# Neighbourhood attention: value products ahead of the next scores, bias tables requested first in each head, on one Trainium2 core

## The chip, the core and the metric

The kernel is one program on one core of a Trainium2 chip. Five instruction streams run side by side and meet only at semaphores: TensorE (PE: matrix products and transposes), VectorE (DVE), ScalarE (ACT), GpSimd (POOL) and SyncE (SP, which here issues DMAs). The metric is device time in microseconds (us) of one execution. All weights and activations are f32; every product is made from halves in a reduced format (high and low, fp32r), usually three matmuls instead of one.

## The reference, cut to what matters

A first transformer block is followed by a second one of two layers. The last attention, changed here, is the neighbourhood attention on 512 tokens (a grid of 8 rows x 64 columns) with 256 context tokens, 16 heads of width 64. Cut from the reference:

```
s_band = einsum('bqhd,brkhd->bhqrk', q_row, kb) * scale + bias      # bias: learned, by 2-D offset
s_band = where(col_mask, s_band, -inf)                             # 16 columns around the query
s_ctx  = einsum('bqhd,bchd->bhqc', q_row, k_c) * scale
p      = softmax(concatenate([s_band, s_ctx], -1))
o      = einsum(p_band, vb) + einsum(p_ctx, v_c)                   # then  y = o @ wo,  h = h + gate * y
```

After it come an RMS norm, a gated FFN, and the last norm.

## The kernel before, in words

**One iteration j (0 to 7) treats two heads of the model.** Below, "head j" is such a pair; h (0, 1) is the member. The 512 queries are cut into four units x of 128 queries (16 columns x 8 rows). `near_steps` (L2741) is the list of steps that all five engines follow. For a unit the steps are:

- `scores j x`: 24 matmuls (L2914, L2917) of 256 columns into PSUM banks 0 to 3: 256 neighbour keys and 256 context keys for each h.
- VectorE reduces them to negated, biased scores and their minimum (`max`, L3096 and L3099, two instructions for each h; the second reads the bias table `tab`). ScalarE takes the exponential with its sum (`exp`, L2992), VectorE its reciprocal (`inv`, L3105), ScalarE multiplies (`share`, L2997).
- `turn j 2x+h`: four transposes (L2928) of the shares into one PSUM bank, from which ScalarE and VectorE take a high and a low half (`t_hi` L528, `t_lo` L533).
- `values j 2p+h`: for a pair p of units, 10 matmuls (L2941) for each h. ScalarE copies one half (`low`, L3014), VectorE adds the other (`full`, L3121), ScalarE and VectorE split the sum (`o_hi` L528, `o_lo` L533).

**Each head has two halves, p = 0 and p = 1.** Between their steps `place` (L539) lays the rest of the work as filler: the projections of head j+1 (`k`, `q`, `v`: L369 to L371; 512 and 256 columns), the transposes of its values (`turn_v`, L2878, halved by `tv_hi` and `tv_lo`), and the output projection of head j-1 (`out`, four steps of two groups n of three matmuls; L369 to L371 from `whi`), whose results VectorE adds to `hT` (L3081). In the first half the order of the steady state is: turns of units 0, `k` 512 columns, turns of unit 1, `k` 256 columns, scores of units 2 and 3, values of p = 0, `q`. In the second: turns of unit 2, `v` 512, turns of unit 3, `out 0`, `v` 256, scores of units 0 and 1 of head j+1, values of p = 1, `out 1`, `out 2`, `turn_v`, `out 3`, and the turns of head j+1.

**PSUM.** Scores own banks 0 to 3. All else shares banks 4 to 7; `Spare` (L588) gives each step the bank that should be free first by the costs in `NEAR_COST`, and `hold` makes TensorE wait until the bank's last reader has gone (`n_add` for `out`, `n_sum` for values, `n_tv_lo` for `turn_v`). In the second half of head 2 the groups n = 2, 3, 4, 5 get banks 5, 6, 7, 5: group 5 waits until VectorE has added group 2.

**Order on the other engines.** `in_time` (L574) sorts the work of ScalarE, VectorE and GpSimd by planned times: the TensorE time of the step plus an offset from `NEAR_SCALAR`, `NEAR_VECTOR`, `NEAR_GPSIMD`. Each engine works strictly in that order.

**Weights and tables.** A step `split` stands for a chunk of weights: SyncE fetches one (L382), ScalarE makes its high half (L394), GpSimd or VectorE the low half (L405). A step `table` fetches the bias rows of a head by 16 small DMAs (L3168) and lets GpSimd make three masked versions for each h (L3149).

**The end.** For head 7 the output projection is done in two strips of 256 queries (`out3`, eight groups each), with the squares for the next norm (`sq` L2241, `sum` L2254) and a product with ones that sums them (`ones`, L2213 and L2215). The order before is: turns, `out3` strip 0, values of p = 1, `ones` 0, `out3` strip 1, `ones` 1; the FFN follows.

Of the kernel before, what the change touches and what calls it, by code (L numbers as in the profile page):

```python
# [373 lines left out]
def fetch_chunk(K, e, w):  # L374

    i = K.fetch_i
    K.fetch_i += 1
    if i >= len(K.chunks):
        return
    if i >= 2:  # L380
        w.wait_ge(*K.at(K.lo_by.get(i - 2, "wlo_dve"), i - 2))
    e.dma_start(K.view(K.raw[i % 2], i), K.chunks[i][0]).then_inc(*K.dma(f"raw{i % 2}", i))  # L382
# [156 lines left out]
def place(fill, share):  # L539

    out = [([], []) for _ in share]
    total, spent, f = sum(c for c, _ in fill), 0.0, 0
    for u in range(len(share)):
        due = total * sum(share[:u + 1]) / sum(share)
        half = total * (sum(share[:u]) + 0.5 * share[u]) / sum(share)
        while f < len(fill) and spent + 0.5 * fill[f][0] < half:
            out[u][0].append(fill[f][1])
            spent += fill[f][0]
            f += 1
        while f < len(fill) and (u + 1 == len(share) or spent + 0.5 * fill[f][0] < due):  # L550
            out[u][1].append(fill[f][1])
            spent += fill[f][0]
            f += 1
    return out
# [2179 lines left out]
def near_load(j):  # L2734

    k = [(0, ("split", j, "k")), (5.4, ("k", j, 0)), (2.8, ("k", j, 512))]
    v = [(0, ("split", j, "v")), (5.4, ("v", j, 0)), (2.8, ("v", j, 512)), (0.7, ("turn_v", j, 0))]
    return k, [(0, ("split", j, "q")), (5.4, ("q", j, 0))], v


def near_steps():  # L2741
    yield "clear", 0, 0
    yield "table", 0, 0
    yield "first_q", 0, 0
    yield "first_k", 0, 512
    yield "second_q", 0, 0
    yield "split_first", 0, "q"
    yield "second_k", 0, 0
    yield "split_first", 0, "k"
    yield "v", 0, 0  # L2750
    yield "scores", 0, 0
    yield "scores", 0, 1
    yield "v", 0, 512
    yield "turn_v", 0, 0
    yield "loop", 0, 0
    for j in range(8):
        k, q, v = near_load(j + 1) if j < 7 else ([], [], [])
        out = [(1.4, ("out", j - 1, n2)) for n2 in range(4)] if j else []
        split = [(0, ("split", j - 1, "out"))] if j else []
        if j < 7:  # L2760
            fill = k + q + [(0, ("table", j + 1, 0))] + v[0:2] + out[0:1] + v[2:3] + split + out[1:3] + v[3:] + out[3:]
            spread = place(fill, NEAR_SHARE)
        else:
            spread = [(split + out[0:1], []), (out[1:2], []), (out[2:4], []), ([], []), ([], []), ([], [])]
            spread = [([s[1] for s in first], []) for first, _ in spread]
        for p in range(2):
            parts = [first + second for first, second in spread[3 * p:3 * p + 3]]
            for h in range(2):
                yield "turn", j, 4 * p + h
            yield from parts[0]  # L2770
            for h in range(2):
                yield "turn", j, 4 * p + 2 + h
            yield from parts[1]
            if p == 0 or j < 7:
                for u in range(2):
                    yield "scores", j + p, 2 * (1 - p) + u
            else:
                yield "out3", 7, 0
            for h in range(2):
                yield "values", j, 2 * p + h  # L2780
            yield from parts[2]
    yield "split_first", 7, "out"
    yield "ones", 7, 0
    yield "out3", 7, 1
    yield "ones", 7, 1


NEAR_SHARE = [1, 0.5, 1, 1, 0.5, 1]
NEAR_COST = {**END_COST, "first_q": 2.9, "first_k": 5.8, "second_q": 2.9, "second_k": 2.9, "q": 5.4, "turn_v": 0.8, "out": 1.4, "scores": 0.95,
             "turn": 0.45, "values": 1.2}  # L2790

# [43 lines left out]
def near_tensor(K, e, w):  # L2835
    wqkv, wo = K.A["na_wqkv_2"][0], K.A["na_wo_2"][0]
    held, spare = {}, Spare(near_steps(), near_cost, near_chain)
    K.named("n_start")
    for what, j, x in spare:
# [111 lines left out]
def near_scalar(K, e, w):  # L2951
    def bank(*key):
        return K.bank(K.xbank[("n",) + key])
    for what, j, x in in_time(near_steps(), near_cost, NEAR_SCALAR, near_chain):
        (qh, ql), (kh, kl), vv = K.nq[j % 2], K.nk[j % 2], K.nv[j % 2]
        if what == "split":
# [85 lines left out]
def near_vector(K, e, w):  # L3042
    def bank(*key):
        return K.bank(K.xbank[("n",) + key])
    for what, j, x in in_time(near_steps(), near_cost, NEAR_VECTOR, near_chain):
        (qh, ql), (kh, kl), vv = K.nq[j % 2], K.nk[j % 2], K.nv[j % 2]
        if what == "split":
# [108 lines left out]
def near_sync(K, e, w):  # L3156
    fetch_chunk(K, e, w)
    w.wait_ge(*K.at("wlo_dve", K.chunk_of["n_start"] - 1))
    for what, j, x in near_steps():
        if what == "table":  # L3160
            w.wait_ge(*K.was("n_max", j - 2, 3, 1))
            if j == 1:
                w.wait_ge(*K.at("norm_lo", "n", KC - 1, 2))
            for h in range(2):
                t = K.tab[j % 2][h][:, 0, :].rearrange("p (r q) -> p r q", q=32)
                for r in range(8):
                    rows = bass.AP(K.rpbd, ((2 * j + h) * 15 + r) * 128 + 40, [[1, 16], [128, 8], [1, 32]])
                    e.dma_start(t[16 * r:16 * r + 16, :, :], rows).then_inc(*K.dma(f"table_in{h}", j, r))  # L3168
        elif what in ("split", "split_first"):
            if K.fetch_i > K.chunk_of["n_end"]:  # L3170
                w.wait_ge(*K.at("n_max", 6, 3, 1))
            fetch_chunk(K, e, w)
# [60 lines left out]
def sync_program(K, e, w):  # L3233
    f0, f1, f2 = feeds(K)
    prelude_sync(K, e, w)
    mixers_sync(K, e, w)
    mixed_sync(K, e, w)
    ffn_sync(K, e, w, f0)
    tail_sync(K, e, w, f0)
    diff_sync(K, e, w)  # L3240
    ffn_sync(K, e, w, f1)
    tail_sync(K, e, w, f1)
    near_sync(K, e, w)
    ffn_sync(K, e, w, f2)
    tail_sync(K, e, w, f2)
# [103 lines left out]
```

## Time and profile before

| | us |
|---|---|
| median of 3 runs | 2666.27 |
| lowest, highest | 2665.56, 2669.49 |
| the profiled execution | 2657.69 |
| its span | 2655.9 |
| TensorE busy | 2474.9 (93%) |
| VectorE busy | 1564.7 (59%) |
| ScalarE busy | 1060.6 (40%) |
| GpSimd busy | 321.1 (12%) |

The span runs from the first to the last instruction that the profile records. The profiled execution took 1.8 us more than its span, and is itself 8.6 us under the median of the three runs. TensorE carries the kernel. The neighbourhood attention lies between about 1865 and 2286 us of the span; there TensorE is busy for 368.6 us of 421.

### The profile page before, as it was taken

The page shows a single profiled execution, that of the slowest core. Times are in us where ns is not written, and L with a number is a line of the kernel's source. Part 1 is how long each engine was busy: PE and PEld are TensorE (multiplying, and loading weights), DVE is VectorE, ACT ScalarE, POOL GpSimd, SP SyncE. Part 2 cuts the span into 40 slices and gives each one's busy share as a digit, 9 for nine tenths or more (in the row PEclk, how much of TensorE's full clock was granted, in tenths as well). Part 3 has the DMA queues.
Part 4 walks back from the last instruction along what each step waited for, and adds up shares of the span by engine and source line. Part 5 has one row for each costly group of instructions (what it writes and reads, how often), then busy time and mean ns, then how long its engine had stood idle before and what let it go on. Part 6 is the DMA issues. An engine that isn't in the chain of part 4 may idle for free.

```text
span 2655.9 us, 35953 instructions
## 1 busy us (share of the span) xinstructions
PE 2474.9 (93%) x14147; PEld 2127.4 (80%) x14147; DVE 1564.7 (59%) x3016; ACT 1060.6 (40%) x1888; POOL 321.1 (12%) x231
## 2 busy tenths in 40 slices
PE   7999989999997999998799999999889988899998
PEld 6888777788787877786688888889878877788887
DVE  4555556878877777777756444445645456533334
ACT  5455534222235655555621211213555555422223
POOL 2122100000012222211100000001232322000001
PEclk9999889999998999999899999999999999899999
DMA  4111023455441111111133333331122211232231
GB/s 122 41 48 48 25 96 111 155 166 182 153 136 48 33 41 40 35 38 48 48 104 122 109 107 127 100 121 55 44 50 55 52 52 52 76 99 95 94 112 49
DMA packets 236577, 218.56 MB, mean 82 GB/s; under 512 B 26164, under 2 KB 205146, under 8 KB 236410
## 3 DMA queue, kind: packets, MB, share of 16 engines
q1 hardware_dynamic: 236410, 216.27, 26.6%
q8 instruction: 113, 1.85, 0.3%
q14 instruction: 54, 0.44, 0.1%
HBM read 214.01 MB, written 2.22 MB: 81 GB/s over the span
## 4 chain that ended last, share of the span: by engine, by line
PE 73%; DVE 13%; ACT 8%; issue 5%; POOL 1%; SPq 0%; DMA 0%; DVEq 0%; POOLq 0%; ACTq 0%
PE ps L369 23%; PE ps L370 22%; PE ps L371 22%; ACT whi L394 1%; DVE FR L533 1%; PE ps L2476 1%; PE ps L2928 1%; ACT FA L2569 1%; DVE FA L667 1%; DVE hT L2649 1%; ACT FR L528 1%; DVE wlo L405 1%; DVE FA L2689 1%; ACT FA L2997 1%; PE ps L2941 1%
## 5 line engine op out<-in xcount | busy, mean ns | idle before, releaser
L369 PE MATMUL ps<-Uh,whi 128*128 128x512 f32 (+2 forms) x2544 | 899.6, 354 | 17.9 <-ACT FA L2588 5.9
L370 PE MATMUL ps<-Ul,whi 128*128 128x512 f32 (+2 forms) x2544 | 885.2, 348 | 0.0
L371 PE MATMUL ps<-Uh,wlo 128*128 128x512 f32 (+2 forms) x2544 | 884.9, 348 | 0.0
L369 PEld LDWEIGHTS ps<-Uh,whi 128*128 128x128 f32 x2544 | 488.6, 192 | 83.1 <-issue 13.7
L371 PEld LDWEIGHTS ps<-Uh,wlo 128*128 128x128 f32 x2544 | 487.2, 191 | 59.6
L370 PEld LDWEIGHTS ps<-Ul,whi 128*128 128x128 f32 x2544 | 488.5, 192 | 57.2
L394 ACT ACTIVATE whi<-raw 128x1024 fp32r<-128x1024 f32 (+2 forms) x205 | 296.5, 1447 | 530.2 <-PE ps L371 530.0
L405 DVE TENSOR_TENSOR wlo<-raw,whi 128x2048 fp32r<-128x2048 f32 (+2 forms) x121 | 248.4, 2053 | 264.3 <-ACT whi L394 264.1
L369 PE MATMUL ps<-FR,whi 128*128 128x512 f32 (+1 forms) x864 | 301.1, 349 | 14.4 <-DVE wlo L405 4.8
L370 PE MATMUL ps<-FR,whi 128*128 128x512 f32 (+1 forms) x864 | 298.3, 345 | 0.0
L371 PE MATMUL ps<-FR,wlo 128*128 128x512 f32 (+1 forms) x864 | 297.9, 345 | 0.0
L405 POOL TENSOR_TENSOR wlo<-raw,whi 128x1024 fp32r<-128x1024 f32 x84 | 201.5, 2399 | 646.2 <-ACT whi L394 645.5
L533 DVE TENSOR_TENSOR FR<-ps,FR 128x512 fp32r<-128x512 f32 (+7 forms) x284 | 142.4, 533 | 145.8 <-ACT FR L528 144.6
L2169 POOL TENSOR_TENSOR FA<-FA 128x256 f32<-128x256 f32 x63 | 49.9, 806 | 1379.4 <-ACT FA L2049 1378.3
L528 ACT ACTIVATE FR<-FA 128x512 fp32r<-128x512 f32 x100 | 58.4, 584 | 351.6 <-DVE FA L1844 343.5
L667 DVE SCALAR_TENSOR_TENSOR FA<-FA,cond 128x512 f32<-128x512 f32 x280 | 196.9, 744 | 1.3
L369 PEld LDWEIGHTS ps<-FR,whi 128*128 128x128 f32 x864 | 164.2, 190 | 37.1 <-ACT whi L394 4.9
L528 ACT ACTIVATE FR<-ps 128x512 fp32r<-128x512 f32 (+7 forms) x304 | 131.2, 467 | 126.8 <-PE ps L371 78.7
L371 PEld LDWEIGHTS ps<-FR,wlo 128*128 128x128 f32 x864 | 164.2, 190 | 19.8
L370 PEld LDWEIGHTS ps<-FR,whi 128*128 128x128 f32 x864 | 164.3, 190 | 19.3
L369 PE MATMUL ps<-whi 128*128 128x512 f32 (+1 forms) x208 | 86.8, 417 | 48.5 <-DVE hT L3081 28.6
L1844 DVE TENSOR_TENSOR FA<-ps,FA 128x512 f32<-128x512 f32 x88 | 54.8, 623 | 115.9 <-PE ps L371 114.4
(352 smaller groups left out, 3041.0 us busy)
## 6 DMA issues: line engine op xcount, KB each, us to landing
FA<-in_ada_w_dram SPq DMA_DIRECT2D x192, 256.0 KB, 2.8
raw<-in_ffn_w_gate_up_dram SPq DMA_DIRECT2D x44, 1024.0 KB, 5.1
raw<-in_ffn_w_down_dram SPq DMA_DIRECT2D x24, 768.0 KB, 4.2
raw<-in_w_in_dram SPq DMA_DIRECT2D x29, 512.0 KB, 3.9
raw<-in_da_wqkv_dram SPq DMA_DIRECT2D x24, 512.0 KB, 3.7
raw<-in_na_wqkv_dram SPq DMA_DIRECT2D x24, 512.0 KB, 3.7
raw<-in_w_ffn_gate_dram SPq DMA_DIRECT2D x11, 1024.0 KB, 5.3
raw<-in_w_ffn_up_dram SPq DMA_DIRECT2D x11, 1024.0 KB, 5.5
```

The costliest lines, as they stand in the source:

```text
L369: e.matmul(out, ah, bh, start=start, stop=False)
L370: e.matmul(out, ah, bl, start=False, stop=False)
L371: return e.matmul(out, al, bh, start=False, stop=stop)
L394: e.activation(K.view(K.hi[i % 2], i), K.view(K.raw[i % 2], i), ACT.Copy).then_inc(*K.ev("whi", i))
L405: e.tensor_tensor(K.view(K.lo[i % 2], i), K.view(K.raw[i % 2], i), K.view(K.hi[i % 2], i).bitcast(F32), ALU.subtract).then_inc(*K.ev(by, i))
L528: e.activation(hi, src, ACT.Copy, scale=scale).then_inc(*K.ev(*done))
L533: e.tensor_tensor(lo, src, hi.bitcast(F32), ALU.subtract).then_inc(*K.ev(*done))
L667: e.scalar_tensor_tensor(out=o, in0=wv, scalar=K.cond[:, k, c:c + 1], in1=o, op0=ALU.mult, op1=ALU.add).then_inc(*K.ev("ada", i, c))
L1844: e.tensor_tensor(mt, K.bank(4 + m % 2)[:, 0:t1 - t0], K.sil[:, m % 2, 0:t1 - t0], ALU.mult).then_inc(*K.ev("f_mul", st, m))
L2169: e.tensor_tensor(acc, acc, K.st_sq4[:, k, :], ALU.add).then_inc(*K.ev("pool_sum", f.st, n, i, z))
L2476: t = e.matmul(K.ps[:, 1024 * mp + c0:1024 * mp + c0 + a1 - a0], q[r:r + 64, q0:q0 + P], k[r:r + 64, a0:a1], start=n == 0, stop=n == 2)
L2569: e.activation(Pm, Pm, ACT.Exp, bias=st[:, 0:1], scale=-1.0, accum_out=st[:, 1:2]).then_inc(*K.ev("d_exp", j, x, mp))
```

## The change

It exchanges two steps in both halves of each head (values first, then the scores of the next two units), requests the next head's bias table as the first filler of a head, with a wait of SyncE on GpSimd's last table, and changes the shares by which the filler is spread.

```diff
-            fill = k + q + [(0, ("table", j + 1, 0))] + v[0:2] + out[0:1] + v[2:3] + split + out[1:3] + v[3:] + out[3:]
+            fill = [(0, ("table", j + 1, 0))] + k + q + v[0:2] + out[0:1] + v[2:3] + split + out[1:3] + v[3:] + out[3:]
...
             yield from parts[1]
+            for h in range(2):
+                yield "values", j, 2 * p + h
             if p == 0 or j < 7:
                 for u in range(2):
                     yield "scores", j + p, 2 * (1 - p) + u
             else:
                 yield "out3", 7, 0
-            for h in range(2):
-                yield "values", j, 2 * p + h
             yield from parts[2]
...
-NEAR_SHARE = [1, 0.5, 1, 1, 0.5, 1]
+NEAR_SHARE = [0.7, 0.8, 1, 0.7, 0.8, 1]
...
             w.wait_ge(*K.was("n_max", j - 2, 3, 1))
+            w.wait_ge(*K.was("n_table", 2 * j - 1))
```

In the steady heads the filler keeps its places. In head 0 the `k` step of 256 columns moves behind the scores in both versions, so values follow the turns directly after the change. In head 7, `out3` of strip 0 now follows the values.

TensorE, second half of head 2, before. L2914 and L2917 are the scores, L2941 the values, the first row the end of `v`, the last the start of `out 1`.

```order
L371 MATMUL ps<-Uh,wlo 128x256
L2914 MATMUL ps<-FR 128x256 x6
L2917 MATMUL ps<-FR 128x256 x6
L2914 MATMUL ps<-FR 128x256 x6
L2917 MATMUL ps<-FR 128x256 x6
L2941 MATMUL ps<-FR 128x256 x6
L2941 MATMUL ps<-FR 128x128 x4
L2941 MATMUL ps<-FR 128x256 x6
L2941 MATMUL ps<-FR 128x128 x4
L369 MATMUL ps<-whi 128x512
```

The same place after.

```order
L371 MATMUL ps<-Uh,wlo 128x256
L2941 MATMUL ps<-FR 128x256 x6
L2941 MATMUL ps<-FR 128x128 x4
L2941 MATMUL ps<-FR 128x256 x6
L2941 MATMUL ps<-FR 128x128 x4
L2914 MATMUL ps<-FR 128x256 x6
L2917 MATMUL ps<-FR 128x256 x6
L2914 MATMUL ps<-FR 128x256 x6
L2917 MATMUL ps<-FR 128x256 x6
L369 MATMUL ps<-whi 128x512
```

The 20 matmuls of the values now stand ahead of the 24 of the scores. The banks move too: the groups n = 2, 3, 4, 5 now get banks 4, 6, 7, 5, of which 5 is that of the values; `turn_v` gets 4 and 6, the groups 6 and 7 get 5 and 7 (in odd heads with 4 and 5 exchanged).

ScalarE, second half of head 2, before. L2979 is the copy of `v`, L2992 `exp`, L2997 `share`, L394 the chunk's high half, L3014 `low`, L528 from FA `o_hi`, the last two rows `tv_hi`.

```order
L2979 ACTIVATE FA<-ps 128x256
L2992 ACTIVATE FA,stat<-FA,stat 128x512 x4
L2997 ACTIVATE FA<-FA,stat 128x512 x2
L394 ACTIVATE whi<-raw 128x1024
L3014 ACTIVATE FA<-ps 64x256 x2
L2997 ACTIVATE FA<-FA,stat 128x512 x2
L528 ACTIVATE whi<-FA 128x8x32
L528 ACTIVATE FR<-ps 128x4x2x64
L528 ACTIVATE FR<-ps 128x3x2x64
```

The same place after.

```order
L2979 ACTIVATE FA<-ps 128x256
L3014 ACTIVATE FA<-ps 64x256 x2
L528 ACTIVATE whi<-FA 128x8x32
L394 ACTIVATE whi<-raw 128x1024
L2992 ACTIVATE FA,stat<-FA,stat 128x512 x4
L2997 ACTIVATE FA<-FA,stat 128x512 x4
L528 ACTIVATE FR<-ps 128x4x2x64
L528 ACTIVATE FR<-ps 128x3x2x64
```

The copy, its half and the chunk now stand ahead of the exponentials. On VectorE, `full` goes ahead of the four reductions, `o_lo` between those of the two units, and the additions of groups 2 and 3 behind them, ahead of the reciprocals.

VectorE, end of head 7, before. L2269 adds the groups of strip 0, L2254 sums squares, L405 is the low half of the FFN's first chunk, L3121 `full`, L533 from FA `o_lo`.

```order
L2269 SCALAR_TENSOR_TENSOR hT<-ps,mod,hT 128x8x32 x5
L2254 TENSOR_TENSOR FA<-FA 128x256
L2269 SCALAR_TENSOR_TENSOR hT<-ps,mod,hT 128x8x32 x2
L2254 TENSOR_TENSOR FA<-FA 128x256 x2
L405 TENSOR_TENSOR wlo<-raw,whi 128x2048
L3121 TENSOR_TENSOR FA<-ps,FA 64x2x8x16 x2
L533 TENSOR_TENSOR wlo<-FA,whi 128x8x32
```

The same place after.

```order
L2269 SCALAR_TENSOR_TENSOR hT<-ps,mod,hT 128x8x32
L3121 TENSOR_TENSOR FA<-ps,FA 64x2x8x16 x2
L2269 SCALAR_TENSOR_TENSOR hT<-ps,mod,hT 128x8x32 x2
L533 TENSOR_TENSOR wlo<-FA,whi 128x8x32
L2269 SCALAR_TENSOR_TENSOR hT<-ps,mod,hT 128x8x32 x3
L2254 TENSOR_TENSOR FA<-FA 128x256
L2269 SCALAR_TENSOR_TENSOR hT<-ps,mod,hT 128x8x32
L405 TENSOR_TENSOR wlo<-raw,whi 128x2048
L2269 SCALAR_TENSOR_TENSOR hT<-ps,mod,hT 128x8x32
L2254 TENSOR_TENSOR FA<-FA 128x256 x2
```

The chunk's low half now stands ahead of the last addition and of the last two sums of squares, on which `ones` 0 waits; ScalarE has the chunk's high half between its fifth and sixth square. SyncE requests the next table ahead of the chunk fetches of a head instead of behind the second one, and GpSimd makes it behind the first low half of a head instead of behind the third.

## Rows read from the trace of the kernel before

**Rows 1.** Waits of TensorE, 1890 to 2290 us: total, times, longest.

```profile
PE ps L369 <- DVE hT L3081: 28.6, 7, 4.2
```

**Rows 2.** Windows: six second halves (heads 1 to 6), scores start to next projection; sum.

```profile
sum 97.93, PE 73.42 PEld 62.55 DVE 61.56 ACT 56.75 POOL 14.11; mean PE 12.24 PEld 10.42 DVE 10.26 ACT 9.46 POOL 2.35
```

**Rows 3.** Timeline of TensorE, second half of head 2: start, us, instruction, wait.

```profile
2026.17 0.50 PE L2914 MATMUL ps<-FR,whi 64*128 64x256 f32 x4
2027.79 2.52 PE L2941 MATMUL ps<-FR 128*128 128x256 f32 x20
...
2030.15 0.45 PE L369 MATMUL ps<-whi 128*128 128x512 f32 x1
...
2036.49 0.80 PE L369 MATMUL ps<-whi 128*128 128x512 f32 x1 [4.05 <-DVE hT L3081]
...
2042.76 0.47 PE L369 MATMUL ps<-Uh,whi 128*128 128x512 f32 x1
```

**Rows 4.** Timeline of VectorE, the same stretch.

```profile
2027.28 0.42 DVE L3096 CUSTOM_DVE_ANT_0 FA<-ps,zero 128x256 f32<-128x256 f32 x1 [2.33 <-issue]
...
2034.78 0.88 DVE L3121 TENSOR_TENSOR FA<-ps,FA 64x256 f32<-64x256 f32 x2 [2.88 <-ACT FA L3014]
2035.69 1.41 DVE L3081 SCALAR_TENSOR_TENSOR hT<-ps,mod,hT 128x512 f32<-128x512 f32 x2
...
2039.66 1.16 DVE L533 TENSOR_TENSOR FR<-ps,FR 128x512 fp32r<-128x512 f32 x2 [0.73 <-ACT FR L528]
```

**Rows 5.** Timeline of ScalarE, the same stretch.

```profile
2031.61 1.32 ACT L2997 ACTIVATE FA<-FA,stat 128x512 f32<-128x512 f32 x2
2032.83 1.04 ACT L394 ACTIVATE whi<-raw 128x1024 fp32r<-128x1024 f32 x1
2033.90 0.78 ACT L3014 ACTIVATE FA<-ps 64x256 f32<-64x256 f32 x2
...
2039.03 1.13 ACT L528 ACTIVATE FR<-ps 128x512 fp32r<-128x512 f32 x2 [2.69 <-PE ps L2878]
```

**Rows 6.** Windows: us, busy time of the engines, PEclk, DMA share, GB/s.

```profile
2036.49:2042.00 5.51, 5.51 (x17) 4.46 (x18) 4.25 (x7) 1.09 (x2) 0.00 (x0) 0.51 0.32 95
...
1901.40:1903.63 2.23, 0.00 (x1) 0.00 (x1) 0.20 (x2) 2.23 (x6) 0.00 (x0) 1.00 0.01 4
...
1278.70:1281.40 2.70, 0.72 (x3) 0.33 (x3) 0.99 (x3) 1.55 (x4) 0.00 (x0) 0.88 0.00 0
```

**Rows 7.** Timeline of TensorE, first half of head 3.

```profile
2053.77 2.53 PE L2941 MATMUL ps<-FR 128*128 128x256 f32 x20
...
2061.67 0.60 PE L2928 MATMUL ps<-ident,FA 128*128 128x128 f32 x4
```

**Rows 8.** Timeline of VectorE, first half of head 3: the first reduction.

```profile
2054.02 0.41 DVE L3096 CUSTOM_DVE_ANT_0 FA<-ps,zero 128x256 f32<-128x256 f32 x1
```

**Rows 9.** Timeline of ScalarE, first half of head 3: the first shares.

```profile
2058.34 1.32 ACT L2997 ACTIVATE FA<-FA,stat 128x512 f32<-128x512 f32 x2
```

**Rows 10.** Timeline of TensorE, second half of head 0.

```profile
1946.14 1.76 PE L2878 MATMUL ps<-ident,FA 128*128 128x128 f32 x7 [5.90 <-ACT FA L2979]
```

**Rows 11.** Timeline of VectorE, second half of head 0.

```profile
1935.37 0.43 DVE L3096 CUSTOM_DVE_ANT_0 FA<-ps,zero 128x256 f32<-128x256 f32 x1 [5.67 <-POOL FA L3149]
```

**Rows 12.** Timeline of TensorE, head 7 from the last scores.

```profile
2235.19 0.51 PE L2914 MATMUL ps<-FR,whi 64*128 64x256 f32 x4
...
2249.25 0.56 PE L369 MATMUL ps<-whi 128*128 128x256 f32 x1
...
2261.31 0.58 PE L369 MATMUL ps<-whi 128*128 128x256 f32 x1 [4.12 <-DVE wlo L533]
```

**Rows 13.** Timeline of ScalarE, end of head 7.

```profile
2255.34 1.89 ACT L394 ACTIVATE whi<-raw 128x2048 fp32r<-128x2048 f32 x1
```

**Rows 14.** Timeline of VectorE, end of head 7.

```profile
2257.27 2.29 DVE L405 TENSOR_TENSOR wlo<-raw,whi 128x2048 fp32r<-128x2048 f32 x1 [1.05 <-ACT whi L394]
```

**Rows 15.** Timeline of SyncE, head 2: the requests of a table.

```profile
2009.30 9.28 SPq L3168 DMA_DIRECT2D FA<-rpb_rows  x16
```

## The prediction

> **What bounds the kernel now.** I first read the page: TensorE is busy for 93% of the span and is the chain that ended last, so only its waits and its clock can give time back. The view of waits, cut to the attention that is changed, names one large item: seven waits of about 4 us, 28.6 us in all, of a group of the output projection on VectorE's addition [rows 1]. The windows of the six second halves that have it (heads 1 to 6), each from the start of the scores to the next head's projection, sum to 97.93 us, a mean of 16.3 [rows 2]. Then the timelines of one of them, engine by engine. TensorE: scores at 2026.17, values at 2027.79 (1.62 later), `out 1` at 2030.15 (2.36 later); three groups, then 4.05 idle until 2036.49, and from there 6.27 to the next projection [rows 3]. VectorE: the reductions start 1.1 after the scores do; `full` comes only at 2034.78, and the addition that frees the bank at 2035.69 [rows 4]. ScalarE says why: `low` at 2033.90 stands behind the exponentials, a share pair (1.32) and a chunk (1.04) [rows 5]. The wait is thus a bank held through a queue, and values issued earlier could shorten it. Last, the clock: in the 5.5 us behind the wait the granted clock is 0.51, the 1.2 GHz level [rows 6].
>
> **Second halves, heads 1 to 6.** I lay the new order on the durations of rows 3 to 5, with V, the end of `v` (2026.17 in rows 3), as zero. TensorE: values 0 to 2.36, scores to 3.98. ScalarE: `low` 2.47 to 3.25, `o_hi`, chunk to 5.65, then four exponentials at a pitch of about 0.87. VectorE: `full` 3.35 to 4.2; two pairs of reductions at 0.87 to 5.9; `o_lo` to 6.3 (256 columns; 0.35 is an estimate from 1.16 for two of 512 in rows 4); two more to 8.0; additions of groups 2 and 3 (1.41) to 9.4; reciprocals to 9.8; additions 4 and 5 to 11.2. ScalarE's shares then lie at 9.6 to 12.2 (twice 1.32), and `tv_hi` (1.13) at 12.2 to 13.3, since it is queued behind them.
>
> TensorE meanwhile: four groups at 0.69 (2.06 for the three before the wait), to 6.74; group 5 has the bank of the values, free at 4.2, and no longer waits. `turn_v` does: its first bank is that of group 2, added at 8.7, its second that of group 3, 9.4. It waits about 2.05, then 0.2, and ends at 9.9. Group 6 has the bank of group 5, added at 11.2: 1.4 of idle. Groups 6 and 7 end at 12.7. The turns of the next head need the two banks of `turn_v`, halved by VectorE at 13.5 and 14.1: 0.9 and 0.2 idle, ending at 14.6; the next projection has group 6's bank, added at 14.8. It starts at V + 14.9. So one wait of 4.05 becomes some five that sum to nearly 5, none over 2.1; what is saved is what the clock cost.
>
> At full clock a half then takes 14.9 against 16.3: 1.4 saved. Will the clock hold? The trace has both. Through a single wait of 2.23 it stayed at 1.00; in a stretch of 2.70 us with 0.72 busy, ahead of a wait of 1.93, it fell (0.88 in the mean) [rows 6]. Here TensorE is busy for some 3 of the 8 us from V + 6.7 on, nearer to the second row. I take it that it falls in most heads, about 3 us into the stretch. In rows 3 the work behind the wait (6.27) would take about 3.7 at full clock by its own warm groups (three groups at 0.69, and an estimate of 0.1 for each of 15 transposes), so the lower level costs up to 2.6 there. Here most of groups 6 and 7 at the lower level hides behind `tv_hi`; what reaches into turns and projection is 0.2 to 2.5, and I take 0.9. Gain 0.5 a head, 3.0 for six. Bounds: 6 x 1.4 = +8.4 with no fall, 6 x -1.1 = -6.6 with the longest one.
>
> The Trainium skill, "TensorE: Matmul & The Clock Gate", section "A second HAM failure mode: psum-queue depth-cycling", tells of a kernel in which short idle times between groups, from cycling through PSUM banks, made the clock go up and down, with the loss paid between bursts. That speaks against breaking one wait into five; by that rule the six halves would bring nothing or lose, by my 0.9 they still bring 3.0. The row of the 2.23 us wait does not bear it out alone, that of the 2.70 us stretch does.
>
> **First halves, heads 1 to 6.** Before, scores are followed by values and `q`, 7.90 in all, until the turns [rows 7]. The reductions start 1.9 after the scores [rows 8], the shares 4.32 after those [rows 9]. After, the turns have only `q` between: scores end at 3.98, `q` (5.53) at 9.5 from the end of `k`. The reductions start behind `full` at 4.15, `o_lo` adds 0.35, so the first share ends at 4.15 + 4.32 + 0.35 + 0.66 = 9.5, the second at 10.15. The turns wait about 0.3. Cost 6 x 0.3 = -1.8; bounds 0 (the spacing absorbs it) and -0.6 each. The cover of the softmax chain is used up here.
>
> **Head 0.** Here TensorE waited 5.90 for the copy of `v` [rows 10], because the first reduction waited 5.67 for GpSimd's late table [rows 11]. With the table requested two fetches earlier both go. Next in line is ScalarE, with the copy behind `low`, `o_hi`, four exponentials and a share: 10.5 against an arrival of TensorE at 7.0, so 3.9 of waiting with the latency, 2.0 less; and TensorE, whose seven transposes took 1.76 behind the long wait, gets about 0.9 back of the lower level: +2.9. In the first half the values follow the turns with nothing between, and wait 1.2 for `t_lo`; ScalarE has the share of unit 3 and `q` later, which costs the last turn some 0.7 more: -1.9. Together +1.0, bounds -1 and +3.
>
> **Head 7 and the end.** In the first half of head 7 the seventh wait of rows 1 goes and the turns wait for shares and banks. By the schedule above the shares end at 12.2 and the last turn at 13.0 from the start of the values; before it took 14.1 from the start of the scores, 2235.19 to 2249.25 [rows 12]. +1.1 (0 to 2). The end loses. Counted from the last turn (T, 2249.25), strip 1 of `out3` started at T + 12.06 before, after a wait of 4.12 on `o_lo` (rows 12 too). That wait goes, since values come first. But the FFN's chunk, 1.89 on ScalarE [rows 13] and 2.29 on VectorE [rows 14], before stood behind all squares and now stands among them. Values wait 0.9 for `t_lo` and end at T + 3.3, the groups at 6.3; ScalarE's chunk runs 7.8 to 9.7, VectorE's 9.8 to 12.1, the last addition to 12.5, two sums with a square between to 13.8; `ones` 0, and strip 1 at T + 14.3. That is -2.3; bounds -4 and +3 (if the groups or chunk come as early as before, strip 1 could start near T + 9).
>
> **Tables in the steady heads, and the added wait.** The 16 requests take 9.28 of SyncE's time [rows 15]. They now go out behind the fetch of `split out`, about V + 8.5, and end near V + 18, where the next head's first projection is under way; the fetch behind them is of a chunk that is split only two splits later, more than 10 us on. GpSimd, which makes the table, is busy for 12% of the span by the page. The added wait is on a table made a head earlier. I put all at 0; without this cover the fetch would be late by 1 us or so, still ahead of its use. No gain either: in rows 4 the reductions wait for the scores, not for a table.
>
> **Sum.** 3.0 - 1.8 + 1.0 + 1.1 - 2.3 = 1.0 us saved, on the profiled execution 2657.7 to 2656.7. The median of the runs is 8.6 above the profiled one; I carry the saving over to it: 2665.3.
>
> **Rivals.**
> Clock stays up: the broken waits leave it at 1.0 as the 2.23 row does. Then the halves give 8.4 and the sum is 6.4: 2660. Against it: the small busy share of the stretch.
> The stall moves and the clock stays down: this is the slower one. The 1.2 GHz level begins late in the stretch, lasts for 7 us (the 5.5 of rows 6 and some of the wait ahead), and runs into the 24 matmuls of the next projection, which before were mostly behind it. A half then takes 17.4, 1.1 more than now; -6.6 for six, with the other terms -8.6: 2675. It decides from the point where a half takes more than 16.3. For it: the waits end later in the stretch than the one of 4.05 did. Against: all of it would have to fall on work that nothing hides.
> The end does not lose: if VectorE's and ScalarE's chunk halves find slack, the end gives +3 and the sum 6.3: 2660 too.
>
> **Chances.** The forecast 0.52, the clock up 0.20, the end not losing 0.08, the clock down 0.20. A measurement of this kernel can tell about 0.2% (5.3 us) from no change. Parts of the clock-up case end under 5.3, part of the slower one too. So faster 0.26, same 0.57, slower 0.17. The likeliest case by itself holds 2661 to 2670; with the other cases the range is 2657 to 2673.
>
> **What would show it.** Right: no wait of 4 us of group 5 on L3081; instead waits of `turn_v` (L2878) near 2 and of group 6 near 1.4, and of the turns near 1; a second half of 15 to 16.3; waits of L2928 of a few tenths in the first halves; no wait of L3096 on L3149; strip 1 of the end near T + 14 with L405 ahead of the last L2269. Wrong: a second half under 15 or over 17, waits of the turns over 1 us in the first halves, or a wait of a chunk on SyncE's requests.

## The result, and the profile after

| | before | after |
|---|---|---|
| median, us (20 runs each) | 2665.9 | 2674.12 |
| lowest to highest | 2655.31 to 2672.69 | 2667.23 to 2679.97 |
| span of the profiled execution | 2655.9 | 2666.5 |
| first scores of the attention | 1896.64 | 1897.70 |
| first projection of the FFN | 2273.05 | 2282.97 |
| between the two ("the stage") | 376.41 | 385.27 |

The ratio is 1.0032, with a 95% interval of 1.0021 to 1.0043: the change makes the kernel 8.2 us slower, where I had said 1.0 faster. The last row of the table is the yardstick of all that follows. The profiled executions differ by up to 14 us in where the stage begins (1894 to 1908 over all kernels below), although nothing ahead of it was edited; from its first scores on they can be compared to a tenth or two of a us (`b_table` below leaves heads 1 to 6 alone, and its halves repeat those of the kernel before within 0.1). The stage grew by 8.86, about the loss of the medians, so the loss lies in it.

The waits of TensorE in the kernel after, from 1860 to 2310 us (total, times, longest). They answer to [rows 1].

```profile
PE ps L2878 <- DVE hT L3081: 23.2, 6, 3.9
...
PE ps L2928 <- ACT FA L2997: 3.4, 1, 3.4
PE ps L369 <- DVE hT L3081: 3.0, 6, 0.7
```

The seven waits of a group of `out` are gone, as forecast. In their place `turn_v` (L2878) waits six times for the same kind of addition, and for 3.9, not for 2.05. The windows of the six second halves, from the start of the values to the next head's projection, answer to [rows 2]: start and end, length, busy time of PE, PEld, DVE, ACT, POOL, then PEclk, DMA share and GB/s.

```profile
2028.62:2046.01 17.39, 13.05 (x80) 10.88 (x78) 11.96 (x31) 9.43 (x20) 2.37 (x1) 0.81 0.25 46
...
sum 103.41, PE 77.24 PEld 63.90 DVE 71.71 ACT 55.63 POOL 14.22; mean PE 12.87 PEld 10.65 DVE 11.95 ACT 9.27 POOL 2.37
```

103.41 against 97.93: 17.24 a half, where I had 14.9 at full clock and 15.8 with the clock's price. VectorE is busy 71.71 us in them, 10 us more than before, with the same instructions. The idle times don't show this: an instruction has become longer. TensorE, second half of head 2, after ([rows 3] before).

```profile
2028.62 2.44 PE L2941 MATMUL ps<-FR 128*128 128x256 f32 x20
...
2039.51 1.76 PE L2878 MATMUL ps<-ident,FA 128*128 128x128 f32 x7 [3.88 <-DVE hT L3081]
2041.72 0.79 PE L369 MATMUL ps<-whi 128*128 128x512 f32 x1 [0.46 <-DVE hT L3081]
...
2044.45 1.84 PE L2928 MATMUL ps<-ident,FA 128*128 128x128 f32 x8
2046.01 0.51 PE L369 MATMUL ps<-Uh,whi 128*128 128x512 f32 x1
```

V is 2028.62 here; `turn_v` starts at V + 10.9, forecast was V + 8.8. VectorE in the same stretch ([rows 4] before).

```profile
2031.97 0.88 DVE L3121 TENSOR_TENSOR FA<-ps,FA 64x256 f32<-64x256 f32 x2 [4.50 <-ACT FA L3014]
2032.88 0.42 DVE L3096 CUSTOM_DVE_ANT_0 FA<-ps,zero 128x256 f32<-128x256 f32 x1
...
2034.63 2.41 DVE L533 TENSOR_TENSOR wlo<-FA,whi 128x256 fp32r<-128x256 f32 x1
2036.97 0.41 DVE L3096 CUSTOM_DVE_ANT_0 FA<-ps,zero 128x256 f32<-128x256 f32 x1
...
2038.70 1.41 DVE L3081 SCALAR_TENSOR_TENSOR hT<-ps,mod,hT 128x512 f32<-128x512 f32 x2
2040.02 0.34 DVE L3105 RECIPROCAL stat<-stat 128x1 f32<-128x1 f32 x4
```

Up to V + 6.0 (2034.63) each row stands within 0.15 of the forecast schedule. Then `o_lo`, 256 columns, takes 2.41 us. All that follows is 2.0 late: the second unit's reductions, the addition that frees the bank of `turn_v`, the reciprocals, and with them the shares. GpSimd at the same time, and the chunk's high half (`whi`) on ScalarE, from which GpSimd makes the low half (before it stood at 2032.83, between two pairs of shares, [rows 5]).

```profile
2034.39 2.37 POOL L405 TENSOR_TENSOR wlo<-raw,whi 128x1024 fp32r<-128x1024 f32 x1 [12.21 <-ACT whi L394]
```

```profile
2033.21 1.04 ACT L394 ACTIVATE whi<-raw 128x1024 fp32r<-128x1024 f32 x1
```

The chunk's low half on GpSimd starts 0.24 ahead of `o_lo` and ends at 2036.76; `o_lo` ends 0.28 behind it. In all six second halves `o_lo` takes 2.41 or 2.42, in the first halves, where GpSimd is idle beside it, 0.42. The same two in the kernel before:

```profile
2034.02 2.35 POOL L405 TENSOR_TENSOR wlo<-raw,whi 128x1024 fp32r<-128x1024 f32 x1 [10.95 <-ACT whi L394]
```

```profile
2037.01 0.41 DVE L533 TENSOR_TENSOR wlo<-FA,whi 128x256 fp32r<-128x256 f32 x1
```

GpSimd's instruction ended at 2036.37, and `o_lo` began at 2037.01: they missed each other by 0.64 us.

The first halves, the start of head 0 and the end, one row or two each: first half of head 3 ([rows 7] before), head 0 ([rows 10] before), and the end of head 7 with the waits ([rows 12] before).

```profile
2055.35 2.44 PE L2941 MATMUL ps<-FR 128*128 128x256 f32 x20
...
2065.04 1.27 PE L2928 MATMUL ps<-ident,FA 128*128 128x128 f32 x8
2066.07 0.47 PE L369 MATMUL ps<-Uh,whi 128*128 128x512 f32 x1
```

```profile
1946.08 0.98 PE L2878 MATMUL ps<-ident,FA 128*128 128x128 f32 x7 [3.36 <-ACT FA L2979]
```

```profile
2252.70 2.96 PE L2928 MATMUL ps<-ident,FA 128*128 128x128 f32 x16 [3.35 <-ACT FA L2997]
2257.03 4.37 PE L2941 MATMUL ps<-FR 128*128 128x256 f32 x20 [1.37 <-DVE FR L533]
...
2270.67 1.19 PE L2213 MATMUL ps<-FA,ones 128*128 128x256 f32 x2 [4.44 <-POOL FA L2254]
```

The first half of head 3 takes 10.72 from values to projection (10.31 from scores to projection before, by the starts 2052.15 and 2062.46). `turn_v` of head 0 waits 3.36 instead of 5.90 and runs at full speed.

### The profile page after: what moved, and what is told of

The parts are those of the page before. It is cut to its first block, busy times and chain, and to the rows that moved or that the text cites. A ratio compares the mean times of both kernels' runs of the same rounds, so it can differ in the third digit from the quotient of the medians.

```text
span 2666.5 us, 35965 instructions
## 1 busy us (share of the span) xinstructions
PE 2483.8 (93%) x14147; PEld 2128.6 (80%) x14147; DVE 1573.7 (59%) x3016; ACT 1057.8 (40%) x1888; POOL 322.7 (12%) x231
## 3 DMA queue, kind: packets, MB, share of 16 engines
HBM read 214.01 MB, written 2.22 MB: 81 GB/s over the span
## 4 chain that ended last, share of the span: by engine, by line
PE 74%; DVE 13%; ACT 7%; issue 5%; POOL 0%; DMA 0%; SPq 0%; DVEq 0%; POOLq 0%; ACTq 0%
PE ps L369 23%; PE ps L370 22%; PE ps L371 22%; PE ps L2941 1%; PE ps L2928 1%; DVE FR L533 1%; PE ps L2476 1%; ACT FA L2569 1%; ACT whi L394 1%; DVE wlo L533 1%; ACT FR L528 1%; DVE FA L667 1%; DVE hT L2649 1%; DVE wlo L405 1%; DVE FA L2689 1%
## 5 line engine op out<-in xcount | busy, mean ns | idle before, releaser
L394 ACT ACTIVATE whi<-raw 128x1024 fp32r<-128x1024 f32 (+2 forms) x205 | 296.5, 1447 | 530.5 <-PE ps L371 530.4
L405 DVE TENSOR_TENSOR wlo<-raw,whi 128x2048 fp32r<-128x2048 f32 (+2 forms) x121 | 248.5, 2054 | 263.1 <-ACT whi L394 262.8
L369 PE MATMUL ps<-FR,whi 128*128 128x512 f32 (+1 forms) x864 | 301.2, 349 | 14.3 <-DVE wlo L405 4.8
L405 POOL TENSOR_TENSOR wlo<-raw,whi 128x1024 fp32r<-128x1024 f32 x84 | 201.5, 2399 | 657.4 <-ACT whi L394 656.7
L533 DVE TENSOR_TENSOR FR<-ps,FR 128x512 fp32r<-128x512 f32 (+7 forms) x284 | 142.1, 533 | 153.2 <-ACT FR L528 152.3
L528 ACT ACTIVATE FR<-FA 128x512 fp32r<-128x512 f32 x100 | 58.4, 584 | 351.2 <-DVE FA L1844 343.0
L528 ACT ACTIVATE FR<-ps 128x512 fp32r<-128x512 f32 (+7 forms) x304 | 129.6, 465 | 107.1 <-PE ps L371 81.5
L2569 ACT ACTIVATE FA<-FA,stat 128x768 f32<-128x768 f32 (+1 forms) x96 | 75.4, 787 | 93.5 <-DVE stat L2672 93.5
```

Source lines behind the costliest of these rows:

```text
L369: e.matmul(out, ah, bh, start=start, stop=False)
L394: e.activation(K.view(K.hi[i % 2], i), K.view(K.raw[i % 2], i), ACT.Copy).then_inc(*K.ev("whi", i))
L405: e.tensor_tensor(K.view(K.lo[i % 2], i), K.view(K.raw[i % 2], i), K.view(K.hi[i % 2], i).bitcast(F32), ALU.subtract).then_inc(*K.ev(by, i))
L528: e.activation(hi, src, ACT.Copy, scale=scale).then_inc(*K.ev(*done))
L533: e.tensor_tensor(lo, src, hi.bitcast(F32), ALU.subtract).then_inc(*K.ev(*done))
L2569: e.activation(Pm, Pm, ACT.Exp, bias=st[:, 0:1], scale=-1.0, accum_out=st[:, 1:2]).then_inc(*K.ev("d_exp", j, x, mp))
```

## The experiments

**Theory A**: VectorE's `o_lo` and GpSimd's low half of the chunk, both with two inputs and the output in SBUF, exclude one another; the change moved the second onto the first. **Rival B**: the many short waits bring the 1.2 GHz level, and that is the loss. **Rival C**: values ahead of scores lengthen the softmax chain by themselves. Times below are of the stage (before 376.41, after 385.27), each read from one profiled execution; medians are of 12 runs (`b_collide` 8), ratios are to the kernel before with 95% intervals.

| kernel | median, us | ratio | stage |
|---|---|---|---|
| a_wait | 2661.18 | 0.9990 (0.9978 to 1.0003) | 372.38 |
| a_chunk | 2665.52 | 1.0005 (0.9992 to 1.0019) | 381.70 |
| a_pieces | 2662.04 | 0.9995 (0.9982 to 1.0008) | 374.51 |
| a_end | 2671.01 | 1.0025 (1.0013 to 1.0037) | 383.08 |
| b_collide | 2673.53 | 1.0041 (1.0026 to 1.0056) | 383.67 |
| b_table | 2658.59 | 0.9987 (0.9975 to 1.0) | 372.96 |
| b_first | 2670.5 | 1.0024 (1.001 to 1.0038) | 382.10 |
| b_second | 2670.72 | 1.0024 (1.0011 to 1.0037) | 379.92 |
| c_best | 2656.7 | 0.9967 (0.9953 to 0.9981) | 369.19 |
| c_head0 | 2656.44 | 0.9964 (0.995 to 0.9979) | 366.91 |
| c_late | 2653.15 | 0.9959 (0.9946 to 0.9971) | 366.98 |

The names: a_ is the changed kernel with one edit, b_ the kernel before with one, c_ a combination.

**a_wait: the two kept apart.**

```diff
         elif what == "split":
+            if x == "out" and j < 6:
+                w.wait_ge(*K.at("n_o_lo", j + 1, 1))
             w.wait_ge(*K.at(*K.pool_prev))
```

> The changed kernel, with one wait more: in heads 1 to 6 GpSimd begins the low half of the weight chunk (L405) of the second half only when VectorE's o_lo of that half is through, so that the two cannot lie side by side. Theory A (the two instructions, both with all operands in SBUF, exclude one another, and o_lo waits 2.0 us for GpSimd): o_lo takes 0.42 again instead of 2.41, turn_v waits about 2 instead of 3.9, a second half takes 15.0 to 15.6 instead of 17.24, the span falls by 10 to 13 us from 2666.5, ratio to before near 0.998. Rival B (the broken waits bring the 1.2 GHz level, and that is the loss): o_lo is short but the half stays at 17. Rival C (values ahead of scores lengthen the softmax chain by themselves): o_lo is short, but it was beside the path, the half stays at 17.

Measured: the stage is 12.9 shorter than that of the kernel after, 4.0 under the kernel before. VectorE, GpSimd and TensorE in the second half of head 2 (V = 2025.62):

```profile
2031.63 0.42 DVE L533 TENSOR_TENSOR wlo<-FA,whi 128x256 fp32r<-128x256 f32 x1
...
2033.72 1.41 DVE L3081 SCALAR_TENSOR_TENSOR hT<-ps,mod,hT 128x512 f32<-128x512 f32 x2
```

```profile
2032.14 2.36 POOL L405 TENSOR_TENSOR wlo<-raw,whi 128x1024 fp32r<-128x1024 f32 x1 [12.94 <-DVE wlo L533]
```

```profile
2034.52 1.21 PE L2878 MATMUL ps<-ident,FA 128*128 128x128 f32 x7 [1.89 <-DVE hT L3081]
2036.74 0.79 PE L369 MATMUL ps<-whi 128*128 128x512 f32 x1 [1.01 <-DVE hT L3081]
...
2040.37 0.48 PE L369 MATMUL ps<-Uh,whi 128*128 128x512 f32 x1
```

`turn_v` starts at V + 8.9 (forecast 8.8, wait 1.89 for 2.05), and the halves take 14.75 to 15.40, mean 15.1. GpSimd's instruction now lies beside the reductions (L3096, L3099), which keep their 0.42 and 0.48: these read one input from PSUM. Rivals B and C fall. The clock did drop here too, in the windows 2035.5 to 2040.5, and the half was 2.6 shorter all the same:

```profile
2033.00:2035.50 2.50, 0.98 (x7) 0.73 (x7) 2.46 (x11) 1.86 (x5) 1.50 (x1) 1.00 0.00 0
2035.50:2038.00 2.50, 1.49 (x6) 1.07 (x4) 1.18 (x2) 2.50 (x5) 0.00 (x0) 0.66 0.91 232
2038.00:2040.50 2.50, 2.50 (x13) 1.97 (x13) 2.20 (x4) 0.93 (x3) 0.00 (x0) 0.66 0.43 41
```

In the second half of head 1 the granted clock is the same in both kernels, 0.82 after and 0.81 here, and the half is 2.01 shorter, which is what `o_lo` had lost:

```profile
1980.17:1997.57 17.40, 12.89 (x79) 10.47 (x78) 11.96 (x31) 9.43 (x20) 2.37 (x1) 0.82 0.24 45
```

```profile
1979.09:1994.48 15.39, 12.87 (x79) 10.43 (x78) 9.97 (x31) 9.44 (x20) 2.37 (x1) 0.81 0.20 45
```

**a_chunk: ScalarE's chunk half back at its old place.**

```diff
-    for what, j, x in in_time(near_steps(), near_cost, NEAR_SCALAR, near_chain):
+    steps = [("split_out", j, x) if (what, x) == ("split", "out") and j < 6 else (what, j, x) ...]
+    for what, j, x in in_time(steps, near_cost, {**NEAR_SCALAR, "split_out": (("split", 3.0),)}, near_chain):
```

> The changed kernel, but in heads 1 to 6 ScalarE's high half of that chunk (L394) goes back to its old place, behind the first pair of shares. GpSimd's L405 then starts some 5 us later, without a wait of its own. Theory A: o_lo 0.42, the second pair of shares and tv_hi about 1.0 later than without the chunk there, so a second half of 15.8 to 16.4, span 5 to 8 us under 2666.5. Rival B: the half stays near 17. Rival C: the half gets longer than 17.2, since the chunk now lies in the softmax chain.

Measured: halves of 16.05 (five of six) and 15.58, with a new wait of 0.7 of the turns. GpSimd's instruction went to 2044.83 in head 2, `o_lo` at 2038.81 took 0.42, without any added wait. Theory A holds. The gain did not come out as expected, though. The span of this profile (2666.9) is not 5 to 8 us smaller than 2666.5: its stage begins 4.7 later, and the stage itself is only 3.6 shorter. The six halves gave 7.6, but 4.0 went again in the projections behind them. From 2048.85 to the next values, 10.38 us, the granted clock is 0.89; the same stretch in the kernel after (from 2046.01) takes 9.34 at 1.00.

**b_collide: the same collision put into the kernel before.**

```diff
         elif what == "split":
+            if x == "out" and j < 6:
+                w.wait_ge(*K.at("n_o_hi", j + 1, 1))
```

> The kernel before, with one wait more: in heads 1 to 6 GpSimd begins the low half of the chunk of the second half (L405) when ScalarE's o_hi of that half is through, that is together with VectorE's o_lo, where it had ended 0.6 us ahead of o_lo. The instructions of VectorE and TensorE keep their order. Theory A: o_lo takes 2.4 instead of 0.42 in the six halves, tv_lo and the additions of groups 4 and 5 behind it come up to 2.0 later, a second half takes 17 to 18.3 instead of 16.3, the span grows by 5 to 12 us over 2655.9. Rivals B and C, by which o_lo is a bystander: the span stays within 2 us.

VectorE and GpSimd, second half of head 2:

```profile
2046.43 2.05 DVE L533 TENSOR_TENSOR wlo<-FA,whi 128x256 fp32r<-128x256 f32 x1
2048.41 1.40 DVE L3081 SCALAR_TENSOR_TENSOR hT<-ps,mod,hT 128x512 f32<-128x512 f32 x2
```

```profile
2045.84 2.37 POOL L405 TENSOR_TENSOR wlo<-raw,whi 128x1024 fp32r<-128x1024 f32 x1 [13.35 <-ACT whi L528]
```

`o_lo` took 2.05 or 2.06 in all six halves: it began 0.59 behind GpSimd's instruction and ended 0.27 behind its end. The stage grew by 7.3. The order of VectorE and TensorE is that of the kernel before, and no wait of TensorE on GpSimd's low half appeared, so the collision alone costs nearly what the whole change does (8.9). The halves were 16.56 to 18.36, not all 17 or more: three grew by 1.4 to 2.8 and three kept their time within 0.4. The windows of the halves of heads 1 and 2 show what goes with it:

```profile
1987.06:2005.07 18.01, 12.95 (x79) 10.62 (x78) 11.91 (x31) 9.45 (x20) 2.37 (x1) 0.81 0.10 29
2035.59:2052.17 16.58, 11.68 (x78) 9.72 (x78) 11.70 (x31) 9.45 (x20) 2.37 (x1) 0.90 0.11 32
```

In all six halves the groups behind `turn_v` wait for an addition a second time, by 0.81 to 1.63. In the three that grew, the granted clock is 0.81 over the half; in the three that did not, it is 0.90: there it was back at the upper level after that wait (a matmul of the groups takes 0.39 to 0.40; before the change it took mostly 0.63), so that the faster groups made up for most of the delay. The size of a loss can thus depend on the clock even where its cause does not.

**a_pieces: the same work in four instructions.**

```diff
+    n = K.chunks[i][1] * K.chunks[i][2] // pieces
+    for y in range(pieces):
+        t = e.tensor_tensor(K.lo[i % 2][:, y * n:(y + 1) * n], K.raw[i % 2][:, y * n:(y + 1) * n],
+                            K.hi[i % 2][:, y * n:(y + 1) * n].bitcast(F32), ALU.subtract)
...
-            split_lo(K, e, w, "wlo_pool")
+            split_lo(K, e, w, "wlo_pool", 4 if x == "out" and j < 6 else 1)
```

> The changed kernel, but in heads 1 to 6 GpSimd makes the low half of that chunk in four instructions of 256 columns instead of one of 1024, at the same time and with the same data. It tells two readings of the collision apart. Exclusive for the length of an instruction: o_lo waits for the end of one piece at most, so it takes 0.42 plus up to 0.7, and a half 15.3 to 16.0, stage 375 to 378 (changed kernel 385.27). Both slow each other down while they overlap: o_lo stays near 2.4, as it does beside one long instruction, and the stage at 384 to 386.

VectorE and GpSimd, head 2:

```profile
2034.80 0.78 DVE L540 TENSOR_TENSOR wlo<-FA,whi 128x256 fp32r<-128x256 f32 x1
```

```profile
2034.57 2.97 POOL L411 TENSOR_TENSOR wlo<-raw,whi 128x256 fp32r<-128x256 f32 x4 [12.22 <-ACT whi L394]
```

`o_lo` begins 0.23 behind GpSimd's first piece and takes 0.78: it waits for one piece, then runs. GpSimd's pieces take 0.72 to 0.73 and one of them 0.91. The exclusion lasts for an instruction, not for the overlap of two streams. The stage is 374.51, 10.8 better than after and half a us under the range that I had given.

**b_table, b_first, b_second: the parts by themselves.**

```diff
b_table
-            fill = k + q + [(0, ("table", j + 1, 0))] + v[0:2] + out[0:1] ...
+            fill = [(0, ("table", j + 1, 0))] + k + q + v[0:2] + out[0:1] ...
...
+            w.wait_ge(*K.was("n_table", 2 * j - 1))
b_first, b_second: values ahead of scores where the condition holds
+            values_first = p == 0                 # b_first
+            values_first = p == 1 and j < 7       # b_second
```

> The kernel before with the table part of the change alone: the request for the next head's table first in each head, and SyncE's wait. Measured on the trace from the first scores of the attention to the start of the FFN, 376.41 before. Theory: only head 0 changes; the wait of 5.90 ahead of turn_v falls to about 3.4 and the stage to 373.5 to 374.5. In no steady head does a step wait for the moved requests. Rival: the gain of head 0 came with the values ahead of the scores; then the stage stays at 376.4, or the requests ahead of a chunk's fetch cost some tenths in each head.

> The kernel before with values ahead of scores in the first half of each head alone. The turns that follow lose one cover of their softmax chain: 0.4 in each of six heads by the two traces, about the same or a little more in heads 0 and 7: stage 378.5 to 380.5. Rival: the 0.4 was an after-effect of the slow clock left over from the second halves; then under 1 us is lost.

> The kernel before with values ahead of scores in the second half of heads 0 to 6 alone, no added wait of GpSimd, the end as before. Theory A (o_lo collides with L405 as soon as ScalarE's chunk stands ahead of the exponentials): o_lo 2.4 in six halves, halves of 17.1 to 17.4, stage 380 to 382. Rival: the collision needs the first halves or the tables changed as well, then o_lo stays 0.42, halves near 15, and the stage falls to 368 to 370.

b_table: stage -3.45. All of it is head 0, 49.05 from the first scores to its end instead of 52.62, with a wait of `turn_v` of 2.49 (expected 3.4); the other halves keep their times within 0.1. This part is good. b_first: +5.7, more than expected; 3.0 of it is head 0 (55.61), where the first reduction still waits 5.84 for the late table and `turn_v` then 6.59. In heads 1 to 6 each first half takes 0.4 longer, as expected; their second halves, whose order was not edited, differ by -0.6 to +1.2. b_second: +3.5, with halves of 17.29 to 17.40 in all six heads and a wait of `turn_v` of 3.85 to 3.88: the collision needs no other part. The halves cost 6.2, and head 0 gained 2.7 (49.93), for which I had not allowed when I expected 380 to 382.

**a_end: the end in its old order.**

```diff
+            values_first = p == 0 or j < 7
```

> The changed kernel, but at the end, in the second half of head 7, out3 of strip 0 stands ahead of the values again, as before the change. All theories: only the end moves. From the last turn T to strip 1 it takes about 12 instead of 16.9, with 1 us lost again in ones or behind; the FFN starts some 3.7 us earlier, span near 2662.8. If the loss of the end comes from the slow clock or from the head 7 turns instead, under 1.5 us come back.

Measured: 2.19 came back, not 3.7. From the last turn to the FFN it is 25.05 instead of 27.3, where the kernel before needs 23.8. So the order of the end costs 2.2, as the prediction said; the other 1.25 comes with strip 0 of `out3`, whose matmuls here stand behind the wait of the turns (3.35) and run at the 1.2 GHz level. The strip is 1.6 longer, and some of that comes back behind it. The windows of that strip, in this kernel and in the one before:

```profile
2264.01:2269.69 5.68, 5.68 (x24) 5.15 (x25) 4.87 (x11) 2.65 (x7) 1.01 (x2) 0.54 0.00 0
```

```profile
2249.25:2253.37 4.12, 3.67 (x26) 3.46 (x25) 3.93 (x10) 2.37 (x6) 0.70 (x1) 0.89 0.00 0
```

**c_best, c_head0, c_late: what the parts suggest.** All have the early table, the first halves and the end as before, and the wait of a_wait. c_best has values first in the second halves of heads 0 to 6; c_head0 leaves out head 0; c_late also puts `o_lo` behind the second unit's reductions.

```diff
+            values_first = p == 1 and j < 7       # c_best
+            values_first = p == 1 and 0 < j < 7   # c_head0, c_late
...
+    for j in range(1, 7):                         # c_late
+        steps.remove(("o_lo", j, 3))
+        steps.insert(steps.index(("max", j + 1, 1)) + 1, ("o_lo", j, 3))
```

> Tables first, values ahead of scores in the second half of heads 0 to 6 only, GpSimd's low half behind o_lo, the end as before. If the parts add up: 372.38 (changed kernel with the wait) less 2.4 for the first halves and less 2.2 for the end, so a stage of 366.5 to 369, 7 to 10 us under before, ratio about 0.9965. If they do not, because the turns then wait for the same shares and banks as before, 370 to 372.

> As c_best, but head 0 keeps scores ahead of values in its second half too. Head 0 took 50.52 from the first scores in c_best and 49.05 in b_table, which is this order: stage 369.19 - 1.5 = 367.7. If the next head pays it back (its first projections wait for the chunks), 368.5 to 369.5.

> As c_head0, but in the second halves VectorE's o_lo stands behind the reductions of both units instead of between them. The additions of groups 2 and 3 keep their time, since it still stands ahead of them; the exponentials of the second unit come 0.35 earlier, the reciprocals keep their time: no change, stage within 0.7 of c_head0. A loss would show that out 1 to 3 wait for o_lo, which no row of the changed kernel shows.

Stages of 369.19, 366.91 and 366.98. c_best lies 0.2 over the range in which the parts add up. The two last are 9.4 to 9.5 under the kernel before. c_late against c_head0 is no difference on the stage (0.07), as expected; the intervals of their ratios overlap. Both are faster than the kernel before by more than their intervals, if only by 0.4%. The stage of c_late (windows, the columns as above) and the waits that are left in it:

```profile
1905.32:2272.30 366.98, 331.07 (x2106) 285.84 (x2105) 197.40 (x583) 205.08 (x417) 101.58 (x76) 0.93 0.20 52
```

```profile
PE ps L2883 <- DVE hT L3090: 11.3, 6, 1.9
PE ps L369 <- DVE hT L3090: 10.1, 7, 4.1
...
PE ps L369 <- DVE wlo L533: 4.1, 1, 4.1
```

L2883 and L3090 are L2878 and L3081 of the other kernels. The two waits of 4.1 are the seventh of [rows 1] and the one of [rows 12]; they stand where the order of before was kept.

## Why the prediction was wrong, point by point

| term, us saved | forecast | measured in the stage |
|---|---|---|
| second halves, heads 1 to 6 | +3.0 | -5.5 (97.93 to 103.41) |
| first halves, heads 1 to 6 | -1.8 | -2.5 |
| head 0 | +1.0 | +1.7 (52.62 to 50.90) |
| head 7, first half, to the last turn | +1.1 | +0.7 |
| the end, from the last turn | -2.3 | -3.5 (23.8 to 27.3) |
| the stretches between | 0 | +0.2 |
| sum | +1.0 | -8.9 |

- **The step that failed** is "`o_lo` to 6.3", with 0.35 for 256 columns, and all that hangs on it: "its first bank is that of group 2, added at 8.7". The work itself is 0.34 on the schedule, as in a_wait (2031.63 to the next reduction at 2031.97). What is missing is what GpSimd does at that moment. The chunk was in my ScalarE schedule ("chunk to 5.65"), and its consumer is GpSimd, which began at V + 5.8, just ahead of `o_lo`; the schedule for GpSimd had no line. In its place: `o_lo` waits 2.0 for GpSimd, on the path to `turn_v` and to the shares, in six halves. a_wait takes away 12.9 of the stage, 2.15 a half; with it the change saves 4.0 (forecast 1.0), and the halves are 1.2 shorter than before rather than my 0.5.
- **"Meet only at semaphores"**, as I wrote of the five streams at the start, is wrong in this case: here VectorE and GpSimd held each other up where no semaphore stands between them.
- **"GpSimd, which makes the table, is busy for 12% of the span"** was used as cover for the tables. It was right for them, and the wrong measure for the rest: 2.4 us in the wrong place cost 2.0 each time.
- **The clock.** The level fell in the halves, as taken, but it cost less than the 0.9 when the schedule held: a half of 15.1 is 0.2 over the full-clock schedule. The rival "clock down" had the time right (2675, a half of 17.4) by luck and the mechanism wrong, as a_wait shows with the clock down and 14.75 to 15.40. What it says of the level running into the next projection did happen in a_chunk (4.0 us), hardly in the kernel after (0.4).
- **The rule set against the change**, of the Trainium skill's "TensorE: Matmul & The Clock Gate", section "A second HAM failure mode: psum-queue depth-cycling", would by my reading have had the broken waits bring nothing or a loss. The clock did go down in a_wait (0.66 in two windows), but it had gone down behind the single wait too (0.51), and with the collision gone the broken waits brought 1.2 a half: the trace bears out the falling clock and not the loss.
- **First halves.** Forecast 0.3 each, measured 0.4, for the reason given. The view of waits does not list it: in head 3 the turns start 0.16 later behind `q`, and the eight of them last 1.03 instead of 0.79, since the next shares come while they run.
- **Head 0.** Its wait fell to 3.36 (forecast 3.9), the values waited 1.23 (forecast 1.2). Right; but either part of the change does it: b_second, with the table still late, has that wait at 3.40 too, and the table alone (b_table) brings more (3.6) than the whole change there (1.7).
- **Head 7 and the end.** The shares end at 12.2 from the start of the values, as forecast, and the last turn at 13.3 (forecast 13.0). The clock behind that wait of 3.35 had no price: from 2252.70 to 2261.24 the granted clock is 0.60, the values take 4.37 instead of 2.44, and strip 1 starts at T + 16.8, not T + 14.3. Strip 1 and what follows it then take 1.2 less than before. By a_end the order costs 2.2, near my 2.3, which was worked out at full clock; the other 1.25 goes with the clock.
- **Tables and the added wait.** No step waits for either. Right.

## What to carry to other kernels

When an edit moves a piece of work on one engine, follow its consumers to their engines and lay those on the schedule too, GpSimd with them, whatever its share of busy time. Where VectorE and GpSimd both work from SBUF to SBUF, ask which one starts first, and whether the later one stands in a chain; keep them apart by a wait or by another place, or cut the longer one into pieces (another place can cost elsewhere, as in a_chunk). A stall of this kind is not in the view of waits: it is recorded as a longer instruction, so compare the busy time and the mean duration of each line between two profiles before reading the idle times.

## What the runs showed of the hardware

- A VectorE subtraction with both inputs in SBUF (L533, 128x256) took 0.42 alone, 2.41 when it began 0.24 behind a GpSimd subtraction of 2.37, 2.05 when 0.59 behind, and 0.78 when that was cut into four. Beside the uncut instruction it ends 0.27 to 0.28 behind GpSimd's end. Instructions of VectorE with one input in PSUM kept their durations beside the same GpSimd instruction in a_wait (L3096 0.42, L3099 0.48, two of L3081 1.41).
- It goes the other way round as well. At the end of the kernel after, VectorE's chunk half (2267.65) begins first, and GpSimd's sum, 0.73 to 0.78 in the other five, takes 2.22:

```profile
2267.65 2.29 DVE L405 TENSOR_TENSOR wlo<-raw,whi 128x2048 fp32r<-128x2048 f32 x1 [0.35 <-ACT whi L394]
```

```profile
2265.89 0.73 POOL L2254 TENSOR_TENSOR FA<-FA 128x256 f32<-128x256 f32 x1 [0.53 <-ACT FA L2241]
2268.30 2.22 POOL L2254 TENSOR_TENSOR FA<-FA 128x256 f32<-128x256 f32 x1 [1.68 <-ACT FA L2241]
```

- The Trainium skill, "SBUF — State Buffer", section "Who interferes with whom", has it that a VectorE instruction with two SBUF inputs contends with a GpSimd instruction that reads SBUF, and that one with at most one SBUF input does not, outside the 2-port modes. Section "SBUF: two separate sides" of the same page of the Trainium skill has it that the first of the two to start holds the shared port pair for its whole instruction while the other fully blocks. The traces agree with both, with the numbers above. An estimate by that rule, with GpSimd's 2.37 laid on my own schedule, is 14.9 + 2.0 = 16.9 for a second half; the prediction had no such term.
- Left open: why the stage begins anywhere from 1894 to 1908 us in executions of kernels that are the same up to there; no run here was made for it. And what the collision at the end costs: GpSimd's sum ends at 2270.52 and L2213, which waits for it, begins at 2270.67, but no kernel took the collision away alone.
